# One token-routing chain with fewer operations, and a second gather that waits for the first

## The chip, the cores and the metric

The kernel runs on one core of one Trainium2 chip. The metric is the device time of one execution in microseconds (us), the median over several executions. TensorE (PE) does the matrix products, VectorE (DVE) the elementwise work on tiles, ScalarE (ACT) activations and copies out of PSUM, GpSimd (POOL) issues the gathers and scatters by row number, and SyncE (SP) issues all other transfers.

## The reference, cut to what matters

One layer of a decoder is computed for 16 learned and 512 prompt tokens and 8 sample tokens, T = 536 in all: an RWKV/retention mixer, then a mixture of experts, then a last norm. The change touches only the routing of the mixture:

```python
lg = u @ router_group_w + b          # 4 groups, top 1
le = u @ router_expert_w + b         # 4 experts in each group, top 2 of the chosen group
combine = onehot(group) * softmax(top 2) * p_group      # (tokens, 16)
h = silu(u @ w_gate[e]) * (u @ w_up[e]) * combine[e]    # each expert e
out = sum_e h @ w_down[e]
```

Ties are resolved to the lower index (argmax and top_k). Each token therefore goes to two of 16 experts.

## The kernel before, in words

The program has two stages after one another. In the first, one long block, all mixer work runs in an order that a list (`order()`, L198 on) writes out by hand; each engine walks through this list and does its share of each step. The second stage is a loop over rounds (one round, when no expert has more than CAP = 96 tokens) whose body is a block too (L2541, L2546). Between the two stages each engine meets all others: the exit of the first block (`mixer.__exit__`, shown as L2495) is a barrier on semaphores, led by POOL, and behind it each engine loads the number of rounds from memory into a register (L2540) and enters the loop.

The experts' work is laid out as 1536 slots, 96 for each expert, in 12 passes of 128 slots. A pass needs the normalised rows of the tokens in its slots. These rows lie in DRAM (`u_rows`); POOL gathers them with an indirect DMA, row numbers from the tile `ids`, column e for pass e, into one of two buffers `ug`. PE transposes a gathered buffer (L2650), DVE scales and moves it to `ue` (L2835), PE multiplies it with the gate and up weights (L2670), ACT and DVE form the hidden values, PE transposes them (L2679) and multiplies with the down weights (L2704), ACT scales the result (L2754) and POOL adds it to the residual rows `x_rows` in DRAM (L2609). The last three passes are kept in SBUF and finished apart (`late`).

Weights of the experts (2 MB gate and up, L967; 1 MB down, L970) come through SP's queue into six buffers. Experts 0 to 2 and the first part of 3 are loaded in the first stage. In the second stage SP first waits for both first gathers (`q_g[0]`, `q_g[1]`), and only then issues the rest of expert 3 and experts 4 and 5; from expert 6 on each load waits for the pass that frees its buffer.

The number of the row in each slot is what the routing chain makes, at the end of the first stage and in two parts: tiles 0 and 1 of 128 tokens beside the last output products of PE (steps `ranked` and `slotted`), tiles 2 to 4 when the last logits are there (step `route`). The functions are:

- `ranked` (L979): logits, then each logit's rank among the four of its row, by comparing all pairs (`gt`, larger; `eq`, equal with a lower index) and a sum; from the ranks the chosen group `ga`, the two choices `ff` and, as their sum in bf16, `selb`.
- `positions` (L1385, on PE): products of `selb` with a triangle and with ones give how many earlier tokens chose each expert.
- `placed` and `slotted`: the place of each choice in its expert, its slot number `d_f`, the pass that it falls in (`is_pass`), its row in the pass (`row`), and from these a one-hot `onehot` over 128 rows and `to_pass`, the token number in two parts (token in its tile, tile) at its pass.
- `slot_products` (L1069, PE): ten products add these up to the token numbers of all slots in PSUM; `slots_known` (DVE) makes integers of them, `ids`.
- `first_rows` (L1082, POOL): waits for `ids` and gathers passes 0 and 1. Ahead of it, at L1287 and L1288, POOL waits until all five transfers of the normalised rows to DRAM (`u2_out`, L1250) have landed.

While DVE ranks, PE works on `final_state` (L1802), products that make a small output state and that nothing else waits for, and ACT copies rows out of PSUM for SP to send to DRAM (first all `u_rows`, then all `x_rows`).

Of the kernel before, what the change touches and what calls it, by code (L numbers as in the profile page):

```python
# [17 lines left out]
ALU = mybir.AluOpType  # L18
# [3 lines left out]
P = 128  # L22
# [10 lines left out]
C = 64  # L33
# [13 lines left out]
NWE = 6  # L47
UNUSED = 4096
EARLY = 2
LATER = HT - EARLY * P  # L50
# [28 lines left out]
for _name, _w in [("ident", P), ("bones", P), ("ones", P), ("tri", P), ("reset", TP), ("lev", len(LEVELS) * H),  # L79
                  ("lev0", 2 * H), ("eyeh", H), ("own", NB), ("ai", 2 * C), ("tie", 16),  # L80
                  ("valid", TT), ("slot", SLOTS), ("more", ROUNDS - 1), ("split", 4 * TT),
                  ("code", NE), ("edge", NPASS + 1),

                  ("smask", 4), ("sdiag", 2), ("fold", NB), ("cos", T), ("sin", T), ("dec", RH * TP), ("dend", TT * RH)]:
    CON[_name] = (_n, _w)
    _n += _w
# [5 lines left out]
def constants():  # L92
# [38 lines left out]
    put("fold", p[:, None] % 32 == np.arange(NB)[None])  # L131
    put("tie", np.broadcast_to((np.arange(4)[None] < np.arange(4)[:, None]).reshape(-1), (P, 16)))
    put("valid", tok < T)
    put("slot", np.broadcast_to(np.arange(SLOTS), (P, SLOTS)))
    put("more", np.broadcast_to(np.arange(1, ROUNDS) * CAP, (P, ROUNDS - 1)))
    put("split", np.repeat(np.stack(np.broadcast_arrays(p[:, None], np.arange(TT)[None] - UNUSED // P), 2)[:, :, None], 2, 2))
    put("code", np.broadcast_to([CAP * place_of(e) for e in range(NE)], (P, NE)))
    put("edge", np.broadcast_to(np.arange(NPASS + 1) * P, (P, NPASS + 1)))
    return t
# [306 lines left out]
def hybrid_step(nc, I, O):  # L446

    with ExitStack() as ctx:
# [399 lines left out]
        c_w, place, first, d_f, off, row = [at(2 * TT) for _ in range(6)]  # L848
        id_f = at(NPASS)
        slot_in = at(2 * NPASS, 2, NPASS)  # L850
        wsel = at(32)
# [16 lines left out]
        gt = at(NS * 16, NS, 4, 4)  # L868
        eq = at(NS * 16, NS, 4, 4)
        mx = at(NS)  # L870
# [70 lines left out]
        NWEIGH = 17  # L941
        NDV = 33
        z_in = sem("z_in")
# [35 lines left out]
        def ranked(dve, v, run, tt, i):  # L979

            t0, t1 = ((0, EARLY), (EARLY, TT))[i]
            rows = slice(t0 * (1 + NG), t1 * (1 + NG))
            if i:
                dve.wait_ge(d_rt, 2)
                run(v.reciprocal(rstd[:, EARLY:TT], rstd[:, EARLY:TT]), d_rc)
            dve.wait_ge(d_lg, i + 1)
            for t in range(t0, t1):
                n = rows_of(t)
                run(v.scalar_tensor_tensor(lg[0:n, t, :], logits(t, n), rstd[0:n, t:t + 1], bias[0:n], ALU.mult, ALU.add))
            x = ll[:, rows]  # L990
            me = bc(x, 4)
            other = x.unsqueeze(2).broadcast_to(list(x.shape[:2]) + [4, 4])
            tt(gt[:, rows], other, me, ALU.is_gt)
            tt(eq[:, rows], other, me, ALU.is_equal)
            tt(eq[:, rows], eq[:, rows], cc("tie", 4, 4).unsqueeze(1).broadcast_to([P, x.shape[1], 4, 4]))
            tt(gt[:, rows], gt[:, rows], eq[:, rows], ALU.add)
            run(v.tensor_reduce(rank.rearrange("p t r e -> p (t r) e")[:, rows], gt[:, rows], AX.X, ALU.add))
            run(v.scalar_tensor_tensor(ga[:, t0:t1], rank[:, t0:t1, 0, :], 0.5, bc(cc("valid")[:, t0:t1], 4), ALU.is_lt,
                                       ALU.mult))
            for a in range(2):  # L1000
                fv = ff[:, t0:t1, a, :].rearrange("p t (g e) -> p t g e", g=NG)
                run(v.scalar_tensor_tensor(fv, rank[:, t0:t1, 1:1 + NG, :], float(a), bc(ga[:, t0:t1], 4), ALU.is_equal,
                                           ALU.mult))
            tt(selb[:, t0:t1, :], ff[:, t0:t1, 0], ff[:, t0:t1, 1], ALU.add, s=d_sel)

            j = slice(2 * t0, 2 * t1)
            tt(tq[:, t0:t1], ff[:, t0:t1], cc("code").unsqueeze(1).unsqueeze(1).broadcast_to([P, t1 - t0, 2, NE]))
            run(v.tensor_reduce(first[:, j], tq[:, t0:t1].rearrange("p t a e -> p (t a) e"), AX.X, ALU.add))
            run(v.tensor_tensor(first[:, j].rearrange("p (t a) -> p t a", a=2), first[:, j].rearrange("p (t a) -> p t a", a=2),
                                bc(lost[:, t0:t1], 2), ALU.add))  # L1010
# [9 lines left out]
        def slotted(v, run, i):  # L1020
# [3 lines left out]
            nj = 2 * (t1 - t0)  # L1024
            run(v.tensor_tensor(d_f[:, j], place[:, j], first[:, j], ALU.add))
            run(v.tensor_scalar(off[:, j], place[:, j], CAP - 0.5, 4096.0, ALU.is_ge, ALU.mult))
            run(v.tensor_tensor(d_f[:, j], d_f[:, j], off[:, j], ALU.add))
            run(v.tensor_tensor(ge[:, j], bc(d_f[:, j], NPASS + 1), cc("edge").unsqueeze(1).broadcast_to([P, nj, NPASS + 1]),
# [4 lines left out]
            run(v.tensor_reduce(row[:, j], ge[:, j, 1:NPASS], AX.X, ALU.add))  # L1033
            run(v.scalar_tensor_tensor(row[:, j], row[:, j], -float(P), d_f[:, j], ALU.mult, ALU.add))
            v.tensor_tensor(onehot[:, j], cc("slot").unsqueeze(1).broadcast_to([P, nj, P]), bc(row[:, j], P),
                            ALU.is_equal).then_inc(q_oh, 1)

        def slots_known(dve, v, run, reach):

            reach(dve, q_pid, 1, 1)  # L1040
            run(v.tensor_copy(slot_in, bank(6)[:, ID0:ID0 + 2 * NPASS].rearrange("p (a n) -> p a n", a=2)))
            run(v.scalar_tensor_tensor(id_f, slot_in[:, 1, :], float(P), slot_in[:, 0, :], ALU.mult, ALU.add))
            v.tensor_scalar(ids[:, :], id_f, float(UNUSED), None, ALU.add).then_inc(q_id, 1)

        def slots_weighed(dve, v, run):

            run(v.scalar_tensor_tensor(place, off, -2.0, place, ALU.mult, ALU.add))
            run(v.tensor_scalar(place, place, 8192.0 - CAP, None, ALU.add))
            dve.wait_ge(d_ex, 1)
# [19 lines left out]
        def slot_products(pe, reach):  # L1069

            reach(pe, q_tp, 2, 2)
            reach(pe, q_oh, 2, 2)
            for j in range(2 * TT):
                last = nc.tensor.matmul(bank(6)[:, ID0:ID0 + 2 * NPASS], onehot[:, j, :], to_pass[:, j], start=(j == 0),
                                        stop=(j == 2 * TT - 1))
            last.then_inc(q_pid, 1)
# [5 lines left out]
        def first_rows(pool, reach):  # L1082

            reach(pool, q_id, 1, 1)
            pool.nop(nofuse=True)
            for e in range(2):
                gather(pool, e)

# [979 lines left out]
        def _(dve):  # L2068
# [32 lines left out]
            for step in STEPS:  # L2101
# [354 lines left out]
                elif kind == "rt_in":  # L2456
                    run(v.memset(eps2[:, :], EPS))
                    run(v.tensor_scalar(lost[:, :], cc("valid"), -4096.0, 4096.0, ALU.mult, ALU.add))
                    run(v.memset(ssq, 1.0))
# [590 lines left out]
```

## Time and profile before

| | us |
|---|---|
| median of 3 runs | 805.24 (803.61 to 805.51) |
| the profiled execution | 804.1 |
| its span (first to last instruction) | 802.5 |
| PE busy | 774.6 |
| DVE busy | 417.8 |
| ACT busy | 212.3 |
| POOL busy | 39.5 |
| mean granted clock of PE | 0.988 |

The profile is that of one execution. Busy times are sums over the span, so they don't tell what a stretch waits for; the chain of waits does, read backwards from the last instruction. All times in rows are us from the start of the span.

### The profile page before, as it was taken

How to read it: one execution, taken by the hardware profiler on the slowest of the kernel's cores; microseconds unless marked ns; L12 is line 12 of the kernel's file. 1: busy time of each engine (PE TensorE's matmuls, PEld its weight loads, DVE VectorE, ACT ScalarE, POOL GpSimd, SP SyncE). 2: the span in 40 equal slices, each digit the busy share in tenths (PEclk: the TensorE clock that was granted, in tenths of full speed). 3: DMA queues.
4: the chain of work that ended last, by engine and by line, in shares of the span. 5: the costliest groups of instructions: out<-in, count | busy, mean ns of one | idle time of the engine just before them, and what ended most of it. 6: DMA issues, size and time to landing. Idle time of an engine off the chain costs nothing.

```text
span 802.5 us, 20031 instructions
## 1 busy us (share of the span) xinstructions
PE 774.6 (97%) x8560; PEld 533.7 (67%) x8560; DVE 417.8 (52%) x848; ACT 212.3 (26%) x499; POOL 39.5 (5%) x50
## 2 busy tenths in 40 slices
PE   7999999999999999999999999999999779999995
PEld 5877777787767867767777877767878633333331
DVE  4965667588777655654444455446314441011146
ACT  4222222254523403212212233220013411111135
POOL 0000000000000000000000000000000021222221
PEclk9999999999999999999999999999999979999998
DMA  9541432431222101101150112056745689999966
GB/s 329 179 162 50 131 106 71 171 125 53 82 75 81 53 29 56 42 29 56 29 177 29 36 48 82 2 176 259 297 158 210 225 305 416 390 388 388 390 225 224
DMA packets 36678, 127.16 MB, mean 158 GB/s; under 512 B 5827, under 2 KB 16099, under 8 KB 31728
## 3 DMA queue, kind: packets, MB, share of 16 engines
q1 hardware_dynamic: 32560, 115.75, 38.7%
q0 software_dynamic: 4032, 10.15, 4.3%
q8 instruction: 68, 1.11, 0.6%
q14 instruction: 18, 0.15, 0.1%
HBM read 106.80 MB, written 18.68 MB: 156 GB/s over the span
## 4 chain that ended last, share of the span: by engine, by line
PE 91%; DVE 4%; DMA 1%; ACT 1%; issue 1%; POOL 0%; SPq 0%; POOLq 0%; ACTq 0%; DVEq 0%
PE psum L1381 23%; PE psum L1362 12%; PE psum L1739 10%; PE psum L2670 10%; PE psum L1339 4%; PE psum L2704 4%; DVE arena L2086 2%; PE psum L1326 2%; PE psum L1314 2%; PE psum L1582 2%; PE psum L2650 1%; PE psum L1595 1%; PE psum L1479 1%; PE psum L1592 1%; PE psum L1553 1%
## 5 line engine op out<-in xcount | busy, mean ns | idle before, releaser
L1381 PE MATMUL psum<-arena 128*128 128x268 f32 x784 | 189.5, 393 | 0.0
L2086 DVE TENSOR_TENSOR arena<-arena 128x268 f32<-128x268 f32 (+12 forms) x308 | 162.6, 528 | 48.0 <-ACT arena L1838 29.3
L1381 PEld LDWEIGHTS psum<-arena 128*128 128x128 f32 x784 | 145.1, 189 | 37.8 <-issue 11.6
L1838 ACT ACTIVATE arena<-psum 128x268 f32<-128x268 f32 (+7 forms) x215 | 85.5, 406 | 272.1 <-PE psum L1381 146.6
L2086 DVE TENSOR_TENSOR arena<-psum,arena 128x256 f32<-128x256 f32 (+5 forms) x161 | 65.3, 410 | 79.5 <-PE psum L1595 27.5
L1362 PE MATMUL psum<-arena 128*128 128x268 f32 x392 | 104.1, 402 | 0.0
L1739 PE MATMUL psum<-arena 128*128 128x268 f32 x384 | 91.0, 391 | 1.6 <-DVE arena L2086 1.2
L2670 PE MATMUL psum<-arena 128*32 128x512 f32 (+1 forms) x640 | 86.5, 603 | 0.5 <-DVE arena L2835 0.3
L1739 PEld LDWEIGHTS psum<-arena 128*128 128x128 f32 x384 | 71.1, 189 | 17.7 <-issue 3.3
L1362 PEld LDWEIGHTS psum<-arena 128*128 128x128 f32 x392 | 69.6, 189 | 16.8 <-issue 3.1
L2835 DVE TENSOR_TENSOR arena<-psum,arena 128x256 f32<-128x256 f32 (+2 forms) x38 | 24.3, 663 | 101.1 <-ACT arena L2739 90.6
L1838 ACT ACTIVATE arena<-arena 128x268 f32<-128x268 f32 (+10 forms) x121 | 49.5, 454 | 101.4 <-PE psum L1751 57.7
L2670 PEld LDWEIGHTS psum<-arena 128*32 128x32 f32 (+1 forms) x640 | 25.4, 116 | 58.0 <-issue 57.4
L2089 DVE SCALAR_TENSOR_TENSOR arena<-arena 128x536 f32<-128x536 f32 (+7 forms) x71 | 41.6, 585 | 11.9 <-DMA arena<-arena 5.0
L2704 PE MATMUL psum<-arena 128*32 128x512 f32 (+1 forms) x288 | 40.2, 595 | 0.0
L2089 DVE SCALAR_TENSOR_TENSOR arena<-psum,arena 128x268 f32<-128x268 f32 (+2 forms) x23 | 10.4, 450 | 48.7 <-PE psum L1739 41.8
L1339 PE MATMUL psum<-arena 128*128 128x268 f32 x128 | 34.3, 404 | 0.0
L2086 DVE TENSOR_TENSOR arena<-arena,psum 128x268 f32<-128x268 f32 (+4 forms) x39 | 20.9, 537 | 24.4 <-PE psum L1362 17.2
L2089 DVE SCALAR_TENSOR_TENSOR arena<-arena,psum 128x268 f32<-128x268 f32 (+1 forms) x36 | 18.8, 521 | 25.5 <-PE psum L1339 12.4
L1285 POOL MEMSET arena<- 64x256 f32 (+1 forms) x18 | 5.5, 312 | 487.2 <-PE psum L1381 266.5
L1339 PEld LDWEIGHTS psum<-arena 128*128 128x128 f32 x128 | 22.3, 189 | 7.2 <-issue 2.8
L2739 ACT ACTIVATE arena<-psum 128x256 f32<-128x256 f32 x12 | 4.6, 385 | 78.0 <-PE psum L2670 78.0
(228 smaller groups left out, 696.0 us busy)
## 6 DMA issues: line engine op xcount, KB each, us to landing
arena<-in_w_gu SPq DMA_DIRECT2D x16, 2048.0 KB, 19.3
arena<-in_w_in SPq DMA_DIRECT2D x45, 512.0 KB, 4.2
arena<-in_w_dn SPq DMA_DIRECT2D x16, 1024.0 KB, 17.8
arena<-in_w_out SPq DMA_DIRECT2D x2, 2048.0 KB, 14.9
arena<-arena SPq DMA_DIRECT2D x5, 536.0 KB, 5.4
arena<-in_x SPq DMA_DIRECT2D x8, 268.0 KB, 6.0
arena<-arena SPq DMA_DIRECT2D x16, 134.0 KB, 4.4
arena<-in_x SPq DMA_DIRECT2D x1, 2144.0 KB, 14.6
```

The source lines that it names most:

```text
L1314: last = mm(ps, wt[:, i, k, :], xg[:, k, cols(hf)], start=(k == 0), stop=(k == KD - 1))
L1326: last = mm(ps, fill_in(0)[side][:, k // 2, k % 2, :], u[:, k, cols(hf)], start=(k == 0), stop=(k == KD - 1))
L1339: last = mm(ps, bb_tile(m)[:, k, :], ret_o[:, k, cols(hf)], start=(k == 0), stop=(k == NP - 1))
L1362: last = mm(ps, w[:, k // 2, k % 2, :], x[:, k, :], start=(k == 0 and i in (0, 1, 3)), stop=(k == KD // 2 - 1), skip_group_check=i not in ...
L1381: last = mm(ps, w[:, k, :], x[:, k, :], start=(k == 0 and i in (0, 1, 3)), stop=(k == KD // 2 - 1), skip_group_check=i not in (0, 1, 3))
L1739: last = mm(ps, w[:, k, :], x[:, k, cols(hf)], start=(k == 0), stop=(k == nk - 1))
L1838: run(nc.scalar.activation(out, in_, fn, **kw), s)
L2086: run(v.tensor_tensor(out, a, b, op), s)
L2089: run(v.scalar_tensor_tensor(out, a, sc_, b, op0, op1), s)
L2670: last = mm(bank(2 + i % 2)[part], ue[:, i % 2, k, part], w_gu[x % NWE][:, k, :], start=(k == 0), stop=(k == KD - 1))
L2704: last = mm(bank(down_bank(e) + q)[part], hht(e)[:, f, part], w_dn[x % NWE][:, f, 512 * q:512 * q + 512], start=(f == 0), stop=(f == 1))
L2835: v.tensor_tensor(out, x, y, op).then_inc(s, 1)
```

## The change

Two things are changed. First, `first_rows` issues the gather of pass 0, waits until its 16 parts have landed (`q_g[0]`), and only then issues the gather of pass 1. Second, the routing chain is written with fewer operations: ties are resolved by "greater or equal" on the pairs where the other index is the lower one, instead of a separate comparison, product and sum; `selb` comes straight from the ranks, ahead of `ff`; slot numbers and their tables are divided by 4096, so that "lost" is an addition of 1 that one operation can do; the two parts of the token number are added by PE in PSUM (20 products of 12 columns instead of 10 of 24, 8 of them before the second `onehot` is waited for), so that DVE needs one operation to make `ids` instead of three.

```diff
@@ ranked
             tt(gt[:, rows], other, me, ALU.is_gt)
-            tt(eq[:, rows], other, me, ALU.is_equal)
-            tt(eq[:, rows], eq[:, rows], cc("tie", 4, 4).unsqueeze(1).broadcast_to([P, x.shape[1], 4, 4]))
-            tt(gt[:, rows], gt[:, rows], eq[:, rows], ALU.add)
+            tt(gt[:, rows, 2:4, 0:2], other[:, :, 2:4, 0:2], me[:, :, 2:4, 0:2], ALU.is_ge)
+            tt(gt.rearrange("p s a b -> p s (a b)")[:, rows, 4:15:10], x[:, :, 0:4:2], x[:, :, 1:4:2], ALU.is_ge)
...
+            run(v.scalar_tensor_tensor(selb[:, t0:t1, :].rearrange("p t (g e) -> p t g e", g=NG), rank[:, t0:t1, 1:1 + NG, :],
+                                       1.5, bc(ga[:, t0:t1], 4), ALU.is_lt, ALU.mult), d_sel)
             for a in range(2):
...
-            tt(selb[:, t0:t1, :], ff[:, t0:t1, 0], ff[:, t0:t1, 1], ALU.add, s=d_sel)
@@ slotted
-            run(v.tensor_tensor(d_f[:, j], place[:, j], first[:, j], ALU.add))
-            run(v.tensor_scalar(off[:, j], place[:, j], CAP - 0.5, 4096.0, ALU.is_ge, ALU.mult))
-            run(v.tensor_tensor(d_f[:, j], d_f[:, j], off[:, j], ALU.add))
+            run(v.scalar_tensor_tensor(d_f[:, j], place[:, j], 1.0 / UNIT, first[:, j], ALU.mult, ALU.add))
+            run(v.scalar_tensor_tensor(d_f[:, j], place[:, j], CAP - 0.5, d_f[:, j], ALU.is_ge, ALU.add))
@@ slots_known
-            run(v.tensor_copy(slot_in, bank(6)[:, ID0:ID0 + 2 * NPASS].rearrange("p (a n) -> p a n", a=2)))
-            run(v.scalar_tensor_tensor(id_f, slot_in[:, 1, :], float(P), slot_in[:, 0, :], ALU.mult, ALU.add))
-            v.tensor_scalar(ids[:, :], id_f, float(UNUSED), None, ALU.add).then_inc(q_id, 1)
+            v.tensor_scalar(ids[:, :], bank(6)[:, ID0:ID0 + NPASS], float(UNUSED), None, ALU.add).then_inc(q_id, 1)
@@ slots_weighed
-            run(v.scalar_tensor_tensor(place, off, -2.0, place, ALU.mult, ALU.add))
-            run(v.tensor_scalar(place, place, 8192.0 - CAP, None, ALU.add))
+            run(v.tensor_scalar(off, place, CAP - 0.5, -8192.0, ALU.is_ge, ALU.mult))
+            run(v.scalar_tensor_tensor(place, off, 8192.0 - CAP, place, ALU.add, ALU.add))
@@ slot_products
-            reach(pe, q_tp, 2, 2)
-            reach(pe, q_oh, 2, 2)
             for j in range(2 * TT):
-                last = nc.tensor.matmul(bank(6)[:, ID0:ID0 + 2 * NPASS], onehot[:, j, :], to_pass[:, j], start=(j == 0),
-                                        stop=(j == 2 * TT - 1))
+                if j == 0:
+                    reach(pe, q_tp, 2, 2)
+                    reach(pe, q_oh, 2, 1)
+                if j == 2 * EARLY:
+                    reach(pe, q_oh, 2, 2)
+                for a in range(2):
+                    last = nc.tensor.matmul(bank(6)[:, ID0:ID0 + NPASS], onehot[:, j, :], to_pass[:, j, a],
+                                            start=(j + a == 0), stop=(j + a == 2 * TT))
@@ first_rows
-            for e in range(2):
-                gather(pool, e)
+            gather(pool, 0)
+            reach(pool, q_g[0], 8 * NPASS, 16)
+            pool.nop(nofuse=True)
+            gather(pool, 1)
```

Left out are the tables of constants (`slot`, `code`, `edge` divided by 4096, `split` with the tile number times 128, `tie` gone), `lost` of 1 instead of 4096, and the row `-P / UNIT` for `-P`.

## Rows read from the trace of the kernel before

**Rows 1.** The page: busy time, share of the span and instructions of each engine
```profile
PE 774.6 (97%) x8560; PEld 533.7 (67%) x8560; DVE 417.8 (52%) x848; ACT 212.3 (26%) x499; POOL 39.5 (5%) x50
```

**Rows 2.** Chain of waits, 600 to the end: start, length, what
```profile
643.62 4.38 DMA arena<-u_rows,ids
648.04 1.97 PE psum L2650 x8
650.13 8.50 PE psum L2670 x61
...
679.42 0.87 PE psum L2650 x8
...
683.88 7.02 PE psum L2670 x64
```

**Rows 3.** Chain of waits in fine, 642 to 660; q is an engine's sequencer
```profile
642.37 0.18 DVE ids L1043
...
642.58 0.04 POOLq L1090
...
642.77 0.61 issue
643.39 0.03 POOLq L1079
```

**Rows 4.** Line L1250 (`u_rows` to DRAM), the transfer issued at 635.4: to landing
```profile
DMA to landing us min/median/max: 7.1/7.1/7.1
```

**Rows 5.** Timeline of DVE, 628 to 652: start, length, operation, shapes
```profile
633.98 1.74 DVE L2086 TENSOR_TENSOR arena<-arena 128x240 f32<-128x240 f32 x4
...
638.69 0.17 DVE L1026 TENSOR_SCALAR arena<-arena 128x6 f32<-128x6 f32 x1
...
641.95 0.18 DVE L1041 COPY arena<-psum 128x24 f32<-128x24 f32 x1 [0.21 <-PE psum L1074]
```

**Rows 6.** Timeline of PE, 628 to 662: the products that give token numbers
```profile
641.42 0.42 PE L1074 MATMUL psum<-to_pass,onehot 128*128 128x24 bf16 x10 [2.28 <-DVE onehot L1035]
```

**Rows 7.** Line L2495, the block's exit: engine, count, ns, first and last start
```profile
L2495 ACTq EVENT_SEMAPHORE  x2: 17/17/17, 645.3 to 645.5; - x2
L2495 POOLq EVENT_SEMAPHORE  x2: 17/17/17, 645.4 to 645.5; - x2
```

**Rows 8.** Line L2544, PE's first step in the loop
```profile
L2544 PEldq FUSED_REGOPS  x3: 37/37/42, 646.4 to 649.9; - x3
```

**Rows 9.** Timeline of POOL: the gathers of passes 0 and 1
```profile
643.62 1.17 POOL L1079 DMA_INDIRECT arena<-u_rows,ids  x1 [150.44 <-issue]
645.09 1.01 POOL L1079 DMA_INDIRECT arena<-u_rows,ids  x1 [0.31 <-issue]
```

**Rows 10.** DMA issues, 797.7 to 798: a scatter with nothing else under way, to landing
```profile
out_y<-arena,ids POOLq DMA_INDIRECT x1, 3.2
```

**Rows 11.** DMA queues, 630 to 650: packets, MB, share; POOL's queue
```profile
q0 software_dynamic: 288, 0.78, 13.8%
```

**Rows 12.** Windows: length, PE, PEld, DVE, ACT, POOL busy, granted clock, DMA share, GB/s
```profile
645.50:648.00 2.50, 0.00 (x0) 0.00 (x0) 0.00 (x0) 1.28 (x1) 0.60 (x1) 0.50 0.86 226
...
652.00:762.00 110.00, 109.65 (x849) 38.48 (x841) 21.27 (x42) 15.40 (x26) 22.91 (x18) 1.00 1.02 397
```

**Rows 13.** Windows, the first 2.6 us of the first gate and up products
```profile
650.10:652.70 2.60, 2.57 (x13) 0.71 (x17) 2.33 (x10) 0.00 (x0) 0.99 (x1) 0.50 0.81 167
```

**Rows 14.** Timeline of SP: the first weight load of the second stage
```profile
649.62 0.34 SPq L970 DMA_DIRECT2D arena<-in_w_dn  x1
```

**Rows 15.** Line L967 in the window 738 to 738.5 (expert 15), issue and landing
```profile
L967 SPq DMA_DIRECT2D arena<-in_w_gu x1: 328/328/328, 738.2 to 738.2; - x1
...
DMA to landing us min/median/max: 29.8/29.8/29.8
```

**Rows 16.** Timeline of PE: the gate and up products of the last pass
```profile
774.99 7.09 PE L2670 MATMUL psum<-arena 128*32 128x512 f32 x64
```

**Rows 17.** Line L2571, a tile of final rows issued at 774.2: to landing
```profile
DMA to landing us min/median/max: 6.7/6.7/6.7
```

**Rows 18.** Timeline of ACT: the square over that tile
```profile
781.00 1.04 ACT L2767 ACTIVATE arena<-arena 128x1024 f32<-128x1024 f32 x1
```

More of the change, by code:

```diff
@@ L48 @@
 UNUSED = 4096
+UNIT = 4096.0
 EARLY = 2
@@ L79 @@
 for _name, _w in [("ident", P), ("bones", P), ("ones", P), ("tri", P), ("reset", TP), ("lev", len(LEVELS) * H),
-                  ("lev0", 2 * H), ("eyeh", H), ("own", NB), ("ai", 2 * C), ("tie", 16),
+                  ("lev0", 2 * H), ("eyeh", H), ("own", NB), ("ai", 2 * C),
                   ("valid", TT), ("slot", SLOTS), ("more", ROUNDS - 1), ("split", 4 * TT),
@@ L131, in constants @@
     put("fold", p[:, None] % 32 == np.arange(NB)[None])
-    put("tie", np.broadcast_to((np.arange(4)[None] < np.arange(4)[:, None]).reshape(-1), (P, 16)))
     put("valid", tok < T)
-    put("slot", np.broadcast_to(np.arange(SLOTS), (P, SLOTS)))
+    put("slot", np.broadcast_to(np.arange(SLOTS) / UNIT, (P, SLOTS)))
     put("more", np.broadcast_to(np.arange(1, ROUNDS) * CAP, (P, ROUNDS - 1)))
-    put("split", np.repeat(np.stack(np.broadcast_arrays(p[:, None], np.arange(TT)[None] - UNUSED // P), 2)[:, :, None], 2, 2))
-    put("code", np.broadcast_to([CAP * place_of(e) for e in range(NE)], (P, NE)))
-    put("edge", np.broadcast_to(np.arange(NPASS + 1) * P, (P, NPASS + 1)))
+    put("split", np.repeat(np.stack(np.broadcast_arrays(p[:, None], np.arange(TT)[None] * P - UNUSED), 2)[:, :, None], 2, 2))
+    put("code", np.broadcast_to([CAP * place_of(e) / UNIT for e in range(NE)], (P, NE)))
+    put("edge", np.broadcast_to(np.arange(NPASS + 1) * P / UNIT, (P, NPASS + 1)))
     return t
@@ L848, in hybrid_step @@
         c_w, place, first, d_f, off, row = [at(2 * TT) for _ in range(6)]
-        id_f = at(NPASS)
-        slot_in = at(2 * NPASS, 2, NPASS)
         wsel = at(32)
@@ L868, in hybrid_step @@
         gt = at(NS * 16, NS, 4, 4)
-        eq = at(NS * 16, NS, 4, 4)
         mx = at(NS)
@@ L941, in hybrid_step @@
         NWEIGH = 17
-        NDV = 33
+        NDV = 29
         z_in = sem("z_in")
@@ L1033, in slotted @@
             run(v.tensor_reduce(row[:, j], ge[:, j, 1:NPASS], AX.X, ALU.add))
-            run(v.scalar_tensor_tensor(row[:, j], row[:, j], -float(P), d_f[:, j], ALU.mult, ALU.add))
+            run(v.scalar_tensor_tensor(row[:, j], row[:, j], -P / UNIT, d_f[:, j], ALU.mult, ALU.add))
             v.tensor_tensor(onehot[:, j], cc("slot").unsqueeze(1).broadcast_to([P, nj, P]), bc(row[:, j], P),
@@ L2457, in _ @@
                     run(v.memset(eps2[:, :], EPS))
-                    run(v.tensor_scalar(lost[:, :], cc("valid"), -4096.0, 4096.0, ALU.mult, ALU.add))
+                    run(v.tensor_scalar(lost[:, :], cc("valid"), -1.0, 1.0, ALU.mult, ALU.add))
                     run(v.memset(ssq, 1.0))
```

## The prediction

> **What bounds the kernel now.** I read the page first: PE is busy for 774.6 of 802.5 us [rows 1], so the change can only matter where PE stands still or is slow. The page's share says nothing of where that is; the chain of waits does. Followed from the last instruction back, it runs along PE nearly all the way and leaves it between 632 and 648, at the seam of the two stages: logits, DVE's ranking and slot numbers, ten products on PE, `ids`, POOL, 4.38 us of a gather, then transposes and the gate and up products of pass 0 [rows 2]. That seam is what both parts of the change touch. The seam is also where the clock is down: the transposes take 1.97 us where later ones take 0.87, and the first gate and up products 8.50 where later ones take 7.02 [rows 2], at a granted clock of 0.50 (1.2 GHz) for the first 2.6 us [rows 13], against 1.00 (2.4 GHz) later [rows 12].
>
> Then I read the seam in fine, because a wait for several things is put down to the last one only. Three questions: what is second to `ids` in what POOL waits for, who leads from POOL to PE, and what SP waits for.
>
> **Part 1, the shorter routing chain.** Only its second half (tiles 2 to 4) is on the chain; the first half lies beside PE's output products, and costs or gives nothing.
> - Ranks: four operations over 128x240 take 1.74 us, 0.43 each [rows 5]. One stays; the other three become two small ones (60 and 30 elements a partition). A small operation takes 0.17 [rows 5]. Between 0.17 and 0.43 each, so 0.45 to 0.95 us less; I take 0.9, by the small row.
> - Slot number: three operations of 0.17 [rows 5] become two: 0.2 less with its gap.
> - `ids`: a copy of 0.18 from PSUM [rows 5] and one more small operation go: 0.4 less.
> - `selb` moves ahead of two operations; PE gets it earlier, and DVE did not wait for PE's answer before. Nothing.
> - Products: ten of 24 columns took 0.42 us [rows 6], and all waited for the second `onehot`. Now 12 of 12 columns do, 8 go ahead. At most 0.42 x 12/10, 0.1 more; at least 0.1 less.
> - `slots_weighed` keeps its two operations, beside PE's pass 0. Nothing.
>
> Together 1.4 us (0.95 to 1.65): `ids` would be there at 641.15 in place of 642.55 [rows 3]. **But POOL can't use it.** Before it looks at `ids` it must see the normalised rows in DRAM. The transfer issued at 635.4 lands 7.1 us later, at 642.5 [rows 4], and POOL went on at 642.58 [rows 3]. That transfer hangs on ACT's copies and on the DMA queue, and DVE's ranking has no part in it. So of 1.4 us some 0.05 is left: the gather starts at 643.55 in place of 643.62. If the rows landed earlier in another execution, the gain would come through, up to 1.4.
>
> **Part 2, the gather of pass 1 waits.** What it should bring: pass 0's rows without the other gather beside them. From 645.5 to 648.0 the DMA engines moved 226 GB/s x 2.5 us = 0.57 MB [rows 12], while the two gathers together are 0.78 MB, 0.39 each [rows 11], so 0.18 MB of the second went before the last part of the first was in. The bounds for the gather alone: 4.38 us, as now [rows 2]; and the 3.2 us of a scatter with nothing beside it [rows 10], plus 0.2 for POOL's longer issue (1.17 us [rows 9]), 3.4. I take the middle, 3.9: landing at 643.55 + 3.9 = 647.45 (646.95 to 647.95) in place of 648.00.
>
> The Trainium skill has a rule against even this ("DMA: Bandwidth & Descriptors", section "SWDGE vs HWDGE vs iDMA"): all DMAs issued from GpSimd go through the one software queue. By that rule the second gather stands behind the first on each engine and can't slow it, and the landing would stay at 4.38 us, the upper bound above; the sum would be 807.4. The same page's section "Anatomy of one DMA" fits a DMA at 2.0 us plus bytes over 436 GB/s. As an estimate from that page 0.39 MB would take 2.9 us, and the sum would be 805.9; the trace has 4.38 for a first gather and does not show this.
>
> What it costs is what stands behind the waiting instruction on POOL: the second gather and then **the exit of the first block**. That exit is a barrier, and POOL leads it: ACT arrives at 645.3, POOL's event follows at 645.4, and both are let go at 645.5 [rows 7]; PE is in the loop at 646.4 [rows 8], 0.9 us later. Now that is hidden behind the landing at 648.00, with 1.6 us to spare. PE's transposes stand behind the barrier. With the change POOL reaches it only after pass 0 has landed:
> - from the release of POOL to having handed on a gather, 642.58 to 643.39: 0.8 us [rows 3]. Should it be held until POOL's engine has taken the gather, 1.04 (642.58 to 643.62) plus 0.3: 1.3;
> - POOL's event to the release of all, 0.1 [rows 7];
> - PE into the loop, 0.9, and its first transpose 0.05.
>
> PE starts at landing + 1.85 (to 2.35): 647.45 + 1.85 = 649.3 in place of 648.04, **1.3 us later** (bounds 648.8 and 650.3: 0.8 to 2.3). PE is busy from there on, so this goes to the end.
>
> **SP and the weights.** SP waits for both gathers; its first load was at 649.62 [rows 14]. The second gather now starts on POOL at 647.45 + 1.04 = 648.5 and lands 3.4 to 4.5 us later (645.09 to 649.6 was 4.5 [rows 9, 14]): SP starts at about 652.4, 2.8 us later, 1.5 more than PE. From 652 to 762 the DMA engines are full, share 1.02 [rows 12], so lateness stays until the end. The tightest weights, expert 15's, landed at 738.2 + 29.8 = 768.0 [rows 15] and are needed at 774.99 [rows 16]: 7 us of cover, enough for 1.5. The second gather itself is needed after pass 0's products, past 658, and lands at 652.4. No cover has the final rows: the tile issued at 774.2 lands at 780.9 [rows 17] and its square starts at 781.00 [rows 18]. Between 0 and 1.5 us of the lateness can show there; I take 0.4, since the last weights had been almost through when those tiles were issued.
>
> **The clock.** PE idles longer at the seam. It is at 1.2 GHz there already, so nothing more is lost by that; when it rises is not in the change's hand. Were it up from the first transpose on, 1.1 + 1.5 = 2.6 us would be won [rows 2]; were it to rise 2 us later in the products, 1 us lost. I take 0.
>
> **Sum.** 804.1 (the profiled execution) + 1.3 + 0.4 = 805.8. That execution is 1.1 us under the median of the runs, 805.24; on the median's scale it is 806.9.
>
> **Rivals.**
> 1. The seam as forecast, but the price is passed on in full: the landing at its upper bound and POOL held (2.3), and the final rows late by the whole 1.5. The point from which it decides is whether the weights are still coming when SP asks for the final rows. For it: the share of 1.02 and a tile without cover. Against: 7 us of cover on the weights. 805.24 + 3.8 = 809.0, slower.
> 2. The barrier does not hold PE: POOL's exit is signalled while the gather is still waiting. Then PE starts at the landing, 0.55 us (0.05 to 1.05) earlier: 804.7; and with the clock up from the start 2.6 less, 802.1. For it: nothing but that I infer the barrier's order from times; the events at 645.3 to 645.5 speak against it.
> 3. The shorter chain comes through, since the rows lie in DRAM earlier than in this trace: 1.4 us off the forecast, 805.5. Against it: 642.5 and 642.55 are as good as equal, so such executions are not the rule.
> 4. The change does what it says and the wait is free because pass 0 alone lands far earlier; for 1.7 us the gather would have to take 2.2 us, less than any indirect transfer here. Counted with 2.
>
> **How the numbers follow.** A measurement of this kernel can tell about 0.3%, 2.4 us, from no change. Forecast 0.55, own range 805.5 to 808.3; rival 1 0.2; rivals 2 and 4 0.15; rival 3 0.1. Slower by over 0.3% (above 807.7): rival 1 and a fifth of the forecast, 0.31. Faster by over 0.3% (below 802.8): a third of rival 2, 0.05. Within: 0.64. Range 804.0 to 809.3: it holds the forecast's range, most of rival 1 and rival 3.
>
> **What would show it.** The chain of waits after should go gather, POOL's sequencer, L2495, the load of the number of rounds, PE: right if POOL's event of the exit comes after the landing and PE's first transpose 1.8 to 2.4 us after it; wrong if it comes within 0.1. `ids` should be written near 641.1 with POOL going on near 642.5 all the same; wrong if POOL follows `ids`. SP's first load should be near 652.4, with no wait of PE for weights. If the whole is faster, the barrier or the clock is where I was wrong; if slower by over 3 us, the weights.

## The result and the profile after

| | before | after |
|---|---|---|
| median, 21 runs each, in turn | 804.28 (802.84 to 807.92) | 807.62 (805.60 to 809.34) |
| the profiled execution | 804.1 | 806.69 |
| its span | 802.5 | 804.9 |
| mean granted clock of PE | 0.988 | 0.989 |

The ratio after to before is 1.0037, 95% interval [1.0029, 1.0045]: 3.0 us slower. The forecast was 806.9 in a range of 804.0 to 809.3. The time is in the range. Of the forecast's three parts two came as described and one did not. Its own sum for the change was 1.7 us (1.3 + 0.4), not 3.0; that the time fits all the same is in part luck, as said at the end. The two profiled executions are 2.6 us apart (804.1 and 806.69), so they show most of the difference and not all of it.

In the trace after, the whole of stage 1 ended 1.4 us earlier (DVE's reciprocal, the first operation of the last routing step, at 631.53, in the trace before at 632.96). Nothing of the change lies ahead of that point but the first half of the chain, which is beside PE's work, and over the fourteen traces of this study that operation starts anywhere between 631.5 and 634.4. So below I count from the start of the first gather, 643.62 before and 643.09 after. From there to the end of the span it was 158.9 us and is 161.8: 2.9 us more, close to the 3.0 of the runs.

**Part 1.** The timeline of DVE (start, length, operation, idle time before it and its releaser), the reciprocal before and then the trace after, against [rows 5] and [rows 3]:

```profile
632.96 0.18 DVE L985 RECIPROCAL arena<-arena 128x3 f32<-128x3 f32 x1 [3.42 <-ACT arena L1838]
```

```profile
631.53 0.18 DVE L982 RECIPROCAL arena<-arena 128x3 f32<-128x3 f32 x1 [3.42 <-ACT arena L1837]
...
632.56 0.92 DVE L2085 TENSOR_TENSOR arena<-arena 128x240 f32<-128x240 f32 x3
...
639.43 0.17 DVE L1036 TENSOR_SCALAR ids<-psum 128x12 int32<-128x12 f32 x1 [0.16 <-PE psum L1071]
```

From the reciprocal to the end of `ids` it takes 8.07 us instead of 9.59 (632.96 to 642.55): 1.5 less. Four operations over 128x240 in 1.74 became one and two small ones, 0.92 together. But the rows in DRAM are not there yet. The last stores of `u_rows` after (their line, with the one landing time that it gives, and POOL's next step behind the wait for them):

```profile
L1249 SPq DMA_DIRECT2D u_rows<-arena x3: 315/327/327, 632.9 to 634.9; - x3
...
DMA to landing us min/median/max: 8.1/8.1/8.1
```

```profile
L1082 POOLq EVENT_SEMAPHORE  x1: 43/43/43, 642.1 to 642.1; - x1
```

The landing time is that of the second of the three, which was issued at 633.94 and landed at 642.05, after the third; POOL went on at 642.1, 2.5 us after `ids` was written at 639.6. The gain is all slack.

**Part 2.** POOL after (timeline), and the block's exit, L2494 now, against [rows 7] and [rows 9]:

```profile
643.09 1.17 POOL L1076 DMA_INDIRECT arena<-u_rows,ids  x1 [151.32 <-issue]
648.18 1.01 POOL L1076 DMA_INDIRECT arena<-u_rows,ids  x1 [3.93 <-POOLq L2494]
```

```profile
L2494 ACTq EVENT_SEMAPHORE  x2: 17/17/17, 642.0 to 648.1; - x2
L2494 POOLq EVENT_SEMAPHORE  x2: 17/17/17, 648.0 to 648.0; - x2
...
  PE psum L2649: 7.9, 1
  ACT L2738: 7.1, 1
```

ACT was at the barrier at 642.0; POOL's event came at 648.0, 0.7 us after the landing at 647.35, and only then was everyone let go. Before, POOL's was at 645.4, 2.6 us ahead of the landing at 648.00. PE's transposes wait for it now. The chain of waits after (start, length, what), against the 4.38 of DMA and the 1.97 of PE right behind it in [rows 2]:

```profile
648.16 0.93 issue
649.09 1.97 PE psum L2649 x8
651.06 0.12 issue
```

PE starts 1.74 us after the landing (0.04 before), 6.00 after the start of the gather (4.42 before): 1.6 us later. In the stretch between, the DMA engines and PE both stand still (windows: length, busy PE, PEld, DVE, ACT, POOL, granted clock, DMA share, GB/s):

```profile
647.40:649.10 1.70, 0.01 (x1) 0.02 (x1) 0.00 (x0) 0.24 (x1) 0.92 (x1) 0.50 0.00 0
```

The gather without the other beside it landed in 4.26 us, against 4.38 [rows 2]. That is 0.1 less, where I had taken 0.5, and even the 0.1 is within the scatter of the other traces: 4.27 to 4.46 us in four with the second gather right behind it, 4.27 to 4.39 in six where the second one waits for its landing. The Trainium skill ("DMA: Bandwidth & Descriptors", section "SWDGE vs HWDGE vs iDMA") says that all DMAs issued from GpSimd go through the one software queue; by that rule the second gather stands behind the first and can't slow it, and these traces agree, to 0.1 us.

**The third part, the weights and the final rows.** SP after, the first load of stage 2 and the five tiles of final rows, against [rows 14] and, for the final rows, the line before:

```profile
652.61 0.34 SPq L967 DMA_DIRECT2D arena<-in_w_dn  x1
...
775.64 2.18 SPq L2570 DMA_DIRECT2D arena<-x_rows  x5
```

```profile
772.91 2.18 SPq L2571 DMA_DIRECT2D arena<-x_rows  x5
```

From the gather's start the first load is 9.52 after, 6.00 before: 3.5 later. The final rows: 132.55 against 129.29: 3.3 later. So 120 us later the delay is still there. SP asks for the final rows when POOL's last scatter to `x_rows` has landed (L2603; it writes rows that DVE has already added up, and is called the last addition below). That line after, around 769, and L2604, the same line before:

```profile
L2603 POOL DMA_INDIRECT x_rows<-arena,ids x1: 996/996/996, 769.6 to 769.6; - x1
...
DMA to landing us min/median/max: 5.8/5.8/5.8
```

```profile
L2604 POOL DMA_INDIRECT x_rows<-arena,ids x1: 997/997/997, 768.7 to 768.7; - x1
...
DMA to landing us min/median/max: 4.0/4.0/4.0
```

A DMA reports its landing in 16 parts. Of this addition, after, 13 landed between 772.2 and 772.5 and the last three at 774.5, 775.3 and 775.4 (these times are the semaphore's 16 updates in the trace). The last weights issued ahead of it (expert 14, down; L967 after, issued at 743.9) landed at nearly the same time:

```profile
L967 SPq DMA_DIRECT2D arena<-in_w_dn x1: 327/327/327, 743.9 to 743.9; - x1
...
DMA to landing us min/median/max: 30.9/30.9/30.9
```

That is 774.8, and before it was 772.1:

```profile
L970 SPq DMA_DIRECT2D arena<-in_w_dn x1: 328/328/328, 743.0 to 743.0; - x1
...
DMA to landing us min/median/max: 29.0/29.0/29.0
```

There too most parts are through long before: in the trace before 11 of the 16 by 764.5, the last two at 772.0 and 772.1. I infer that the addition's last parts stand behind weights on the same slow DMA engines; a trace doesn't name the engine of a part. The times bear it out. Thirteen traces of this study give both landings. In ten of them the addition took 4.0 to 7.8 us and landed within 0.7 of those weights' last part. In the three where the weights were through no later than 2.2 us after its issue (e4, e5, f1) it took 3.2, the time of a scatter alone [rows 10].

From SP's first load to the landing of those weights the two traces take 122.5 and 122.2 us (649.62 to 772.1; 652.61 to 774.8), and the other twelve 120.6 to 124.9. From there to SP's first tile of final rows it is 0.8 in both. So, by this reading, what counts for the end is two or three DMA engines that are behind the others after 120 us of weights, and a later start of the weights is a later end.

Then it reaches the end. The chain of waits there was ACT's before, coming from PE (L2739 follows the gate and up products of the last pass but one), and is the addition's and the tile's after. Before, then after:

```profile
774.73 0.39 ACT arena L2739
...
781.00 1.14 ACT arena L2767 x2
```

```profile
769.61 5.84 DMA x_rows<-arena,ids
...
776.91 6.66 DMA arena<-x_rows
```

ACT's square over the fourth tile of final rows, and PE's last transposes of the hidden values, after, against [rows 18]:

```profile
783.60 1.06 ACT L2766 ACTIVATE arena<-arena 128x1024 f32<-128x1024 f32 x1 [0.84 <-DMA arena<-x_rows]
```

```profile
787.83 0.44 PE L2678 MATMUL psum<-arena 128*128 128x128 f32 x2 [0.52 <-DVE arena L2834]
```

The square started at 781.00 before without a wait and now waits 0.84 for the tile. From it to the end of the span it is 21.3 us (21.5 before). In the fourteen profiled executions of this study that stretch is 21.3 to 21.5 us in ten, and 22.2 to 22.4 in the four where PE's clock fell behind its last long wait (e3, f5, g1, g2). So the start of that square sets the end of this kernel, but for the clock. Two chains lead to it, and before they were equal to 0.1 us: PE's (ACT comes free, 781.00) and the tile's landing (780.9 [rows 17]). The change delays the first by 1.6 us (by 1.8 at ACT: 778.19 against 776.90 for the first of the squares, from gather to gather) and the second by 3.1 (783.60 - 643.09 = 140.51, against 137.38). The later one sets the end.

### The profile page after: what moved, and what is told of

Read it like the earlier page. It is cut to its first block and busy times, and to the rows that moved or that the text cites. A ratio compares the mean times of both kernels' runs of the same rounds, so it can differ in the third digit from the quotient of the medians.

```text
span 804.9 us, 20046 instructions
## 1 busy us (share of the span) xinstructions
PE 772.8 (96%) x8570; PEld 533.0 (66%) x8570; DVE 415.8 (52%) x842; ACT 212.5 (26%) x499; POOL 39.3 (5%) x50
## 5 line engine op out<-in xcount | busy, mean ns | idle before, releaser
L2085 DVE TENSOR_TENSOR arena<-arena 128x268 f32<-128x268 f32 (+13 forms) x306 | 161.2, 527 | 47.8 <-ACT arena L1837 29.8
L1380 PEld LDWEIGHTS psum<-arena 128*128 128x128 f32 x784 | 145.3, 189 | 37.6 <-issue 11.6
L2669 PEld LDWEIGHTS psum<-arena 128*32 128x32 f32 (+1 forms) x640 | 25.3, 116 | 57.9 <-issue 57.3
L2703 PEld LDWEIGHTS psum<-arena 128*32 128x32 f32 (+1 forms) x288 | 10.8, 115 | 21.3 <-issue 21.3
```

The lines of the kernel that those rows point to most:

```text
L1380: last = mm(ps, w[:, k, :], x[:, k, :], start=(k == 0 and i in (0, 1, 3)), stop=(k == KD // 2 - 1), skip_group_check=i not in (0, 1, 3))
L2085: run(v.tensor_tensor(out, a, b, op), s)
L2669: last = mm(bank(2 + i % 2)[part], ue[:, i % 2, k, part], w_gu[x % NWE][:, k, :], start=(k == 0), stop=(k == KD - 1))
L2703: last = mm(bank(down_bank(e) + q)[part], hht(e)[:, f, part], w_dn[x % NWE][:, f, 512 * q:512 * q + 512], start=(f == 0), stop=(f == 1))
```

## The experiments

Times are medians; ratios are to runs of the kernel before that were taken together with these. A distance in us is the ratio's. In each trace, the places are counted from the start of gather 0.

**e1: the wait alone.** The kernel before with the changed `first_rows`:

```diff
-            for e in range(2):
-                gather(pool, e)
+            gather(pool, 0)
+            reach(pool, q_g[0], 8 * NPASS, 16)
+            pool.nop(nofuse=True)
+            gather(pool, 1)
```

> The kernel before with the second part of the change alone: the gather of pass 1 waits for the landing of pass 0's. My theory: the whole loss is in this part, because the shorter chain ends in front of the landing of the rows in DRAM and gives nothing. Then this kernel stands 3.0 us (0.37%) over the kernel before, as the changed kernel does, within 0.6. Rival: the shorter chain does give its 1.4 us and the wait costs more than it seems; then this kernel stands 4.4 us over the kernel before. In the trace POOL goes on at the writing of ids (some 0.1 us behind it) and PE's first transpose comes 1.75 us after the landing.

Measured: 811.05, ratio 1.0086 [1.0072, 1.0100], 6.9 us slower. Neither expectation holds, though the sign does. Its profiled execution, the fastest of its six, is like the changed kernel's: gathers at 643.16 and 648.31, final rows at 775.81, the square at 784.62. The extra 3 to 4 us are not in that trace; see g1.

**e2: the chain alone.** The changed kernel with both gathers at once (the same lines the other way round).

> The changed kernel with both gathers issued at once, as before: the shorter chain alone. My theory: ids are written 1.5 us earlier, counted from the logits, and POOL still waits for the rows in DRAM; total 0.0 to 0.3 us under the kernel before, no difference that can be measured. Rival (the chain counts): 1.4 us (0.17%) under it.

Measured: 804.37, 0.9996 [0.9986, 1.0006]. The chain gives nothing here. In its trace `ids` was written at 639.98, 8.1 us after the reciprocal (9.59 before), and the gather started where it did before, 0.3 us apart:

```profile
639.81 0.17 DVE L1036 TENSOR_SCALAR ids<-psum 128x12 int32<-128x12 f32 x1 [0.19 <-PE psum L1071]
```

```profile
643.31 1.17 POOL L1076 DMA_INDIRECT arena<-u_rows,ids  x1 [151.19 <-issue]
644.78 1.00 POOL L1076 DMA_INDIRECT arena<-u_rows,ids  x1 [0.31 <-issue]
```

So none of the loss comes from the chain, and the wait alone makes one (e1). That the wait alone loses more than both parts together is taken up at g1.

**e3: the exit's cost taken away.** The changed kernel, with wait and second gather moved behind the block's exit, into POOL's part of the loop:

```diff
@@ first_rows
-            reach(pool, q_g[0], 8 * NPASS, 16)
-            pool.nop(nofuse=True)
-            gather(pool, 1)
@@ POOL in the loop
+                    then(q_g[0], EVERY, 16)
+                    gather(pool, 1)
```

> The changed kernel with the wait for pass 0's rows and the gather of pass 1 moved from the end of the first stage to POOL's first lines in the loop, so that POOL reaches the block's exit without waiting. My theory: PE's first transpose comes right at the landing (0.05 us after it) again, the seam's 1.75 us go, and what is left is the late start of the weights (SP still waits for the second gather, near 652): 1.0 to 1.5 us over the kernel before. Rival: the exit cost nothing, the loss is all from the late weights and final rows; then this one stays 3.0 us over. Second rival: the exit was all of it; then it equals the kernel before.

Measured: 808.71, 1.0047 [1.0033, 1.0061], 3.8 us slower: the rival held. The timeline of PE shows what became of the exit's cost:

```profile
649.59 1.97 PE L2648 MATMUL psum<-arena 128*128 128x128 f32 x8 [4.79 <-DMA arena<-u_rows,ids]
...
790.49 0.44 PE L2677 MATMUL psum<-arena 128*128 128x128 f32 x2 [2.93 <-DVE arena L2833]
790.86 5.35 PE L2702 MATMUL psum<-arena 128*64 128x512 f32 x16
```

PE waits for the data again and not for the barrier, and starts 4.32 after the gather's start (4.42 before): the 1.6 us are won back. SP's first load is as late as in the changed kernel:

```profile
654.80 0.34 SPq L967 DMA_DIRECT2D arena<-in_w_dn  x1
```

9.53 from the gather, against 9.52. The 1.6 us come back as a wait at the end, 2.93 us, behind the final rows. The square starts 140.98 from the gather, in the changed kernel 140.51: with PE on time and the weights late it is no earlier. Then the clock falls besides (granted 0.70 from 790.49 to 796.10, where the trace after has 1.00): 16 products in 5.35 us, where they took 3.66 after a wait of 0.52.

**e4: SP asks for gather 0 only.** The changed kernel, so that weights go beside gather 1:

```diff
-                    for q in range(2):
-                        at_least(sp, q_g[q], EVERY, 16)
+                    at_least(sp, q_g[0], EVERY, 16)
```

> The changed kernel, but SP waits for the first gather only before it issues the rest of the experts' weights, so they start 3.5 us earlier, near 649.2. The second gather then runs beside weights. My theory: the seam's 1.75 us stay, and the waits at the end (for the tiles of final rows, 1.1 us on ACT, and for a gather, 0.4 us on PE) go: 1.5 to 2.0 us over the kernel before. Rival: those waits at the end have another cause (the gathers, or chance): 3.0 us over, no change against the changed kernel.

Measured: 807.28, 1.0027 [1.0014, 1.0039], 2.2 us slower (1.1 to 3.1). SP started 6.35 after the gather, as good as before (6.00), PE remained late by the exit, and gather 1 took its usual 4.3 us, as the weights were issued 1.1 us behind it. The 1.5 to 2.0 expected by the theory lie in the interval, but so does the rival's 3.0. What is left is of the size of PE's 1.6, a little above. Its profiled execution was the slowest of the six, so I draw nothing from its tail.

**e6 and e5: the rows first.** In both, SP sends the rows of tiles 2 to 4 to DRAM ahead of expert 3's 2 MB instead of behind it; e6 is the kernel before with that alone, e5 has the shorter chain too (both gathers at once). If the rows hold POOL back, the chain should now come through:

```diff
-            load_gu(sp, 3)
             for t in range(2, TT):
                 u2_out(t)
+            load_gu(sp, 3)
```

> The kernel before with one order changed on SP's queue: the three stores of normalised rows go ahead of the 2 MB load of expert 3's gate and up weights, so they land some 3 us earlier, well before ids are written. The routing chain and the gathers are as before. Theory: ids (9.6 us after the reciprocal) release the gather as before; the 2 MB now run beside the x rows and into the gathers, which costs 0 to 1 us: 0 to 1.0 us over the kernel before.

> The same order of SP's queue with the shorter routing chain (both gathers at once). It takes the cover of the chain away, the landing of the rows. Theory: the chain's 1.5 us now come through: gather released near 8.2 us after the reciprocal, and the time 1.4 us (0.17%) under the kernel with the rows first and the long chain, 0.4 to 1.4 us under the kernel before. Rival (something else holds the gather, or a fixed end on the DMA side takes it back): no difference between the two kernels with rows first.

Measured: e6 805.52, 1.0022 [1.0010, 1.0033], 1.8 us slower; e5 807.30, 1.0034 [1.0021, 1.0047], 2.7 us slower. Both are slower than expected, and e5, which was to be 1.4 us under e6, is not faster than it. In e6 the rows were in DRAM by 639.1 and `ids` came last, at 642.7. In e5 POOL did start earlier, at 641.93 as against 643.78 in e6. But the gather now flies beside 2 MB of weights. The line of the first gather, e6 and then e5:

```profile
L1079 POOL DMA_INDIRECT arena<-u_rows,ids x1: 1167/1167/1167, 643.8 to 643.8; - x1
...
DMA to landing us min/median/max: 6.0/6.0/6.0
```

```profile
L1076 POOL DMA_INDIRECT arena<-u_rows,ids x1: 1168/1168/1168, 641.9 to 641.9; - x1
...
DMA to landing us min/median/max: 8.1/8.1/8.1
```

The start is 1.8 us earlier and the landing 0.2 later. The chain is worth nothing even where `ids` comes last: next in line are the transfers that it meets, the 2 MB of weights (landed at 646.4 in e5) and the stores of `x_rows` behind them.

**f3 and f4: SP late alone.** By now my theory was that lateness of SP's first load passes to the end 1 to 1. The kernel before, with nothing but SP held back: in f3 until DVE has moved pass 0's rows to `ue`, in f4 until the transfer of `retp` has landed, now issued first:

```diff
@@ f3, ahead of load_dn(sp, 3)
+                    at_least(sp, q_ue, PIECES, 2)
@@ f4
-                    load_dn(sp, 3)
                     sp.dma_start(O["retp"], ret_st).then_inc(z_out[1], 16)
+                    at_least(sp, z_out[1], 48, 16)
+                    load_dn(sp, 3)
```

> The kernel before with one more wait of SP ahead of its first weight load of the second stage: until DVE has scaled pass 0's rows (near 650.7 in place of 649.6, 1.1 us later). PE, POOL, the gathers and the block's exit are as before. New theory: the stage has two chains of equal length, PE's and that of the slowest DMA engine, which is never empty from SP's first load until its last weights (122.3 us later in five of six traces), and on which the final rows and the end wait. Then this kernel stands 1.1 us (0.14%) over the kernel before. Rival (the theory of the prediction: the weights have 7 us of cover and only part shows at the end): 0 to 0.4 us.

> The same with a larger dose: SP issues the small store of the retention state first and waits until it has landed (near 655.3) before its first weight load, 5.6 us later than before. New theory: 5.5 us (0.7%) over the kernel before, since the slowest DMA engine's chain is moved by all of it, and no wait for weights on PE itself before the last pass. Rival (7 us of cover): under 1 us.

Measured: f3 804.67, 1.0002 [0.9994, 1.0011]; f4 804.83, 1.0005 [0.9993, 1.0017]. Both doses were smaller than meant. Counted from the gather, SP's first load was 1.1 us late in f3 (7.07, not 6.00) and 2.5 in f4 (8.48), not 5.6: `retp` landed in 2.4 us on idle DMA engines. The final rows were issued 0.9 and 0.6 later, and the square started 0.9 and 1.2 later; by the runs the whole is 0.2 us slower (-0.5 to 0.9) and 0.4 (-0.6 to 1.4). Both lie where the rival had put them. f3's interval includes nothing and ends just under its dose of 1.1. f4, whose 2.5 us at SP became 0.6 at the final rows, speaks against 1 to 1: its weights took 120.6 us from first load to last landing instead of 122.5, and my guess is that what the DMA engines did in the gap (`retp`) they had not to do later. Neither settles the theory for 3.5 us, so I needed a larger dose.

**f5: SP late by 8.5 us.** The kernel before, SP waits for the gate and up products of pass 0 (`at_least(sp, q_gu, NPASS, 1)`) ahead of `load_dn(sp, 3)`.

> The kernel before with SP's first weight load of the second stage behind the gate and up products of pass 0 (near 658.7 in place of 649.6, 9 us later); nothing else is touched. The two smaller doses moved the slowest DMA engine's end by only 0.5 and 0.8 us, since the transfers of gathers or of the state ran in the gap. This one should move it by about 7 to 8. Theory of two chains: 5.5 to 8 us over the kernel before, with PE waiting only at the last pass, for ACT. Rival (7 us of cover at expert 15): 0 to 2 us over.

Measured: 814.29, 1.0114 [1.0100, 1.0129], 9.2 us slower, with nothing of the change in it; the first gather and PE's start as before, the second gather 0.7 us longer. The theory's 5.5 to 8 was too low, the rival's 0 to 2 far off. SP's first load was 14.54 after the gather, 8.5 later:

```profile
658.46 0.34 SPq L970 DMA_DIRECT2D arena<-in_w_dn  x1
```

So a late start of the weights alone makes the kernel slower, by about its lateness at this dose. PE's timeline shows two waits, of which I had expected only the second:

```profile
742.57 7.07 PE L2671 MATMUL psum<-arena 128*32 128x512 f32 x64
...
758.28 8.69 PE L2671 MATMUL psum<-arena 128*32 128x512 f32 x64 [3.81 <-issue]
...
794.83 0.44 PE L2680 MATMUL psum<-arena 128*128 128x128 f32 x2 [3.65 <-DVE arena L2836]
795.20 5.35 PE L2705 MATMUL psum<-arena 128*64 128x512 f32 x16
```

PE waits 3.81 us ahead of a pass whose weights are late, runs it at a lower clock (8.69 us at a granted clock of 0.81, where the earlier pass took 7.07 at 1.00), waits 3.65 behind the final rows and loses 1.7 by the clock again. The weights waited for are expert 13's. Before, they landed at 748.3 for a pass that started at 754.6, so their cover was 6.3 us, less than the 7 of expert 15's; here they landed at 758.2, 9.6 later counted from the gather.

**f1: both costs taken away.** e3 and e4 together: the exit free, SP behind gather 0 only.

> The changed kernel with both of the costs of its wait taken away at once: the gather of pass 1 (still after the landing of pass 0) stands in POOL's lines in the loop, behind the block's exit, and SP waits for the first gather alone. With the exit free but SP late the time was 3.8 us over the kernel before; with SP early but the exit held 2.2 over. Theory of two chains (PE's and the slowest DMA engine's): each of these left one chain late, and with both taken away it equals the kernel before, within 0.6 us. Rival: the gather of pass 1 beside the weights costs in itself: 1.5 us or more over.

Measured: 807.01, 1.0035 [1.0019, 1.0051], 2.8 us slower: the rival held. SP's first load is earlier than in the kernel before (646.88, 4.29 from the gather), PE starts in time, and now gather 1, issued at 647.72 with the weights already on their way (from 646.88), is late. Its line, and PE's wait for it:

```profile
L1076 POOL DMA_INDIRECT arena<-u_rows,ids x1: 1004/1004/1004, 647.7 to 647.7; - x1
...
DMA to landing us min/median/max: 11.6/11.6/11.6
```

```profile
659.35 1.09 PE L2647 MATMUL psum<-arena 128*128 128x128 f32 x8 [2.16 <-DMA arena<-u_rows,ids]
660.79 8.79 PE L2667 MATMUL psum<-arena 128*64 128x512 f32 x32 [0.35 <-DVE arena L2832]
```

2.16 us of waiting and 1.7 of clock (8.79 at a granted clock of 0.80; the same shape took 7.11 at 768.87 in the trace after). So f1 takes both costs away and puts a new one in their place; it does not show that the two costs are all of the change's.

**g1 and g2: the wait alone and the changed kernel, side by side.** g1 is e1 again, g2 the changed kernel again, to see whether e1's excess was chance.

> The kernel with the wait alone once more, beside the changed kernel on one chip, since the first time it stood 6.9 us over the kernel before where the changed kernel stood 3.0 over. Theory: both have the wait, and the chain ends ahead of the landing of the rows in either, so the difference was one of the chip or of chance: within 1 us of the changed kernel. Rival: with the wait in place the longer chain costs 3 to 4 us more: again 6 to 7 us over the kernel before.

> The changed kernel once more, on the same chip as the one with the wait alone: 3.0 us (0.37%) over the kernel before, within 0.8.

Measured: g1 810.38, 1.0066 [1.0048, 1.0084], 5.3 us slower; g2 806.92, 1.0029 [1.0019, 1.0039], 2.3 slower. The two intervals don't meet, so the excess is real: beside the wait, the shorter chain is worth some 3 us, though alone it is worth nothing. The theory (within 1 us of each other) fell. g1's trace shows how it appears: gather 1 took 5.8 us to land (4.4 in the trace after), SP's first load came 10.95 from the gather (9.52), the weights then took 124.9 us to their last landing (122.2), and it has both of f5's waits:

```profile
756.43 7.09 PE L2672 MATMUL psum<-arena 128*32 128x512 f32 x64 [0.82 <-issue]
...
790.60 0.69 PE L2681 MATMUL psum<-arena 128*128 128x128 f32 x2 [2.88 <-DVE arena L2837]
791.22 4.91 PE L2706 MATMUL psum<-arena 128*64 128x512 f32 x16
```

Why the longer chain makes gather 1 and the weights later is not shown: in g1 as in the trace after, POOL's first gather waited for the rows and not for `ids`. In e1's own trace gather 1 took 4.7 us, in g2's 4.5, so this alone doesn't settle it. It stays open.

## Why the forecast held, and the step in which it was wrong

- **Part 1.** 1.4 us forecast, 1.5 measured; "POOL can't use it" held, and e2 shows it over 11 runs; e1 and g1 show that it is not so beside the wait. Rival 3 (the chain comes through) fell: `ids` leads the rows by 2.5 us in the trace after. I had said "wrong if POOL follows `ids`"; it follows the rows.
- **Part 2, the landing.** 3.9 us taken, 4.26 measured, near the upper bound of 4.38. The bytes that I counted as the other gather's share before the landing did not stand in its way: with and without it the first gather takes 4.3 to 4.5 us.
- **Part 2, the exit.** The barrier is led by POOL, and the order gather, POOL's event, release, PE is as forecast. PE's start at landing + 1.74 (forecast 1.85 to 2.35). Later by 1.6, forecast 1.3: the landing came 0.4 later than taken, the exit took 0.1 less. Rival 2 (the barrier does not hold PE) fell.
- **SP and the weights: the step that failed.** The start, 2.8 later by the forecast, was right in its mechanism and is 3.5 counted from the gather (3.0 in the trace's own times). I took 0.4 of a possible 1.5 for the final rows, "since the last weights had been almost through when those tiles were issued". That was argued from most of the engines, but a DMA has landed when its last part has, and the last two parts came 7.6 us behind eleven of the sixteen (772.1 against 764.5). The weights were indeed through when the tiles were issued (772.1 and 772.9), but only because SP waits for the addition, and the addition landed 0.6 us behind them, before and after (772.7 and 775.45). In the trace after its last parts came 3 us behind the rest. Measured, this term is 3.1 - 1.8 = 1.3 us. With the 1.8 of PE's chain at ACT it makes the 3.1. e3 shows that the two are not a sum but a maximum: with the exit's 1.6 gone the kernel is no faster. The forecast's 1.3 + 0.4 had the form of a sum.
- **Rival 1** named what came true, the rest of SP's lateness in full at the final rows. Its deciding point, "whether the weights are still coming when SP asks for the final rows", was near the mark but not met as it stands: they were through 0.8 us ahead of that, before and after. What the weights made late was the addition, and with it SP's asking. Its price (3.8) was too high as it took both bounds of the exit too. I had set 7 us of cover on the weights against it; that cover was for PE's products, and the final rows were never behind it. Nor was it the tightest: expert 13's weights had 6.3. I gave it 0.2 and should have given it half.
- **The clock** was no term in the trace after: mean granted clock 0.988 and 0.989, and the first products 8.33 against 8.50. It became one in e3, f1, f5 and g1, and also in g2, which is the changed kernel itself: its profiled execution (809.04, the slowest of its eight) waits 1.95 us at the end and then takes 5.35 for the 16 products, at a granted clock of 0.70. So in some executions of the changed kernel the clock is a term that I had put at nothing; in how many is not shown.

Why the time fitted all the same: the rest of the forecast (1.7) stood on a median of three runs, 805.24, which lay 1 us above the median of all 21, 804.28. On that one the forecast would have been 806.0, 1.6 under. The forecast for the changed kernel was 0.7 under what was measured, that of the difference 1.3 under (3.0 by the ratio).

No version here was faster than the kernel before. The nearest is e2, equal to it.

## What to carry to other kernels

Before adding a wait, look at what stands behind it on its queue. Here a wait meant for one gather held a barrier of all engines, and another wait, on SP, for the gather behind it, held the weights of twelve experts; the second cost more though its effect showed 120 us later. When two chains meet at the same instant, as ACT's coming free and the tile's landing did (781.00 and 780.9), a delay costs the maximum of both, not the sum, and shortening one brings nothing. Where the DMA engines are full, read the landing of the last part and not the mean share: cover that holds for one consumer says nothing of the next.

## What was not expected of the hardware

- Of the 16 parts of one DMA the slowest landed far behind the rest after a long full stretch: expert 14's down weights before, the first at 758.0, eleven by 764.5, the last at 772.1. A small scatter issued then took 5.8 us to its last part (4.0 before, 3.2 with nothing beside it [rows 10]).
- A first gather of 0.39 MB took 4.3 to 4.5 us with another gather behind it or none, but 6.0 and 8.1 when issued behind weights (e6, e5), and the second one 11.6 (f1). With the weights issued 1.1 us after it instead, it took 4.3 (e4); with none under way it still took 5.2 once (f5) and 5.8 once (g1).
- PE's waits of 1.95 (g2), 2.16 (f1), 2.9 (e3, g1), 3.65 and 3.81 us (f5) were each followed by slower products, 1.5 to 1.7 us in all; those of 0.4 to 1.6 us (after, e1, e2, e4, e5, f3, f4, g1's first) were not.
